# RWKV-7 layer on one core: a reordered recurrence unit, and an output block with two pairs of heads in work

## Chip, cores and metric

One core of a Trainium2 chip runs the whole program. The metric is the device time of one execution in microseconds. TensorE is abbreviated PE in the profile, VectorE DVE, ScalarE ACT, GpSimd POOL, and SyncE, which here issues most DMAs, SP.

## Reference

One layer of a hybrid trunk over 128 context and 512 latent tokens (T = 640 in all), model width 2048: a modulated RMSNorm, one input projection, three token mixers, an output projection, and an expert-choice feed-forward. The change touches the third mixer, RWKV-7 with 16 heads of 64 channels in two directions, and what follows it:

```python
def step(S, xs):                       # per token, per head, per direction
    r_t, w_t, k_t, v_t, a_t, b_t = xs
    sa = jnp.einsum('bhvk,bhk->bhv', S, a_t)
    S = S * w_t[:, :, None, :] + sa[..., None] * b_t[:, :, None, :] + v_t[..., None] * k_t[:, :, None, :]
    return S, jnp.einsum('bhvk,bhk->bhv', S, r_t)
...
o = outs[0] + outs[1]                  # forward + backward
o = ((o - mu) * lax.rsqrt(var + GN_EPS)) * lp['rw_ln_w'] + lp['rw_ln_b']
bonus = jnp.sum(rf * kf * lp['rw_rk'], axis=-1, keepdims=True) * vf
gate = jax.nn.sigmoid(x_g) @ lp['rw_g2']
return ((o + bonus) * gate), finals[0], finals[1]
```

The mean and variance are over the 64 channels of one head. The latent scan starts from a cached state; the context scan's final state is an output.

## The kernel before

The program is a sequence of blocks; a block ends when all engines have done their part. The two that the change touches are `block_rwkv` (the recurrence) and `block_rwkv_output`.

**The recurrence.** Tokens are cut into 10 chunks of 64 (2 context, 8 latent). A unit u is one direction of one pair of heads: 2 x 8 pairs = 16 units. Each engine runs a written-out list, `LINES[u]`, in its own order; semaphores join them. One line holds:

- the front of unit u + 1: jobs `w`, `a` (PE, emptied by ACT with tanh into `sg` and `ar`), then on DVE `scan` (L1593 adds 1 to `sg`, L1595 is a prefix sum over the tokens), then products on POOL (`front`), exponentials on ACT, and the scaled operands `bk` and `aq`;
- the body of unit u: five score jobs `sc` (PE, emptied and masked by DVE L1573 into `sc`), and the inverse of a triangular matrix by doubling, levels 0 to 4, in two halves b: job `x` (needs the transposed tile `tm`, DVE L1565, and `near`, which ACT cuts from `sc` in L1495), job `d`. POOL prepares the tile that is transposed, in three operations (L1312, L1314, L1316, `start`) that wait for the scores of their half. `far` is used at level 4 only;
- 30 slots for the chains of the units u - 2 ("old", chunks 5 to 9) and u - 1 ("new", chunks 0 to 4), alternating. A chunk has three stages: `pw` (PE: five products, four matmul instructions each, of which two need the state `st`; ACT copies `wsb`), `u` (PE, ACT copies `usb`), `z` (PE; then DVE adds the PSUM result to the state into `tmp`, L1631, and scales it by the decay into `st`, L1638; ACT copies the output, L1535). PE starts the next `pw` of that chain only when L1631 has emptied the bank and L1535 has run. When a chain begins, its first `pw` stage has DVE clear `st` (L1626).

The jobs of the body use a ring of four PSUM banks. The order of one line is written in `plan`; its head is: w0 a0 w1 a1, sc0, two slots, sc1, scan, two slots, sc2, two slots, sc3, two slots, sc4, two slots, turn0, x0, slot, bk0, turn1, x1. After the last unit the chains drain: five chunk steps of two chains, then five of one.

**The output block** does the eight pairs one after another. Per pair, 128 partitions x 640 tokens: SP loads `o`, `r`, `k`, `v` (320 KB each) into two buffers; DVE L1797 makes r*rk*k; PE makes the mean; DVE L1799 subtracts it; ACT squares (L1776); PE makes bonus sum, gate and variance; DVE L1801 multiplies bonus by v; ACT takes Ln and Exp (L1779, L1781); DVE L1803 to L1806 finish in four operations; SP stores. PE and DVE begin the next pair when the last one's L1806 is done. Behind pairs 0, 1 and 2, SP also loads three 1 MB slabs of `w_out` each, ahead of the next pair's loads. POOL writes 5 MB of zeros to `ffn` near the start of the block.

Of the kernel before, what the change touches and what calls it, by code (L numbers as in the profile page):

```python
# [15 lines left out]
F32 = mybir.dt.float32  # L16
# [1051 lines left out]
def block_rwkv(nc, z_d, kk_d, par_d, w2, a2, state, ident_d, o_raw_d, state_out):  # L1068
# [17 lines left out]
    def plan(u):  # L1086
# [4 lines left out]
        then = {(0, 1): ["removal"], (2, 0): ["exp_in"], (2, 1): ["exp_inv"], (3, 0): ["exp_ex", "decay", "pad_b"], (3, 1): ["pad_k"], (4, 0): ["pad_a"]}  # L1091
        items = [w0, a0, w1, a1]
        for b in range(NCK // 2):
            items += [("sc", b, u)] + (["scan"] if b == 1 else []) + ["slot", "slot"]
        for lv in range(LAST_LV + 1):
            for k, kind in enumerate(("x", "d")):
                for b in range(2):
                    items += (["turn%d" % b] if (lv, kind) == (0, "x") else []) + [(kind, b, lv, u), "slot"]
                    items += [fill[lv][k]] if lv in fill and b == 0 else []
                items += then.get((lv, k), [])  # L1100
# [35 lines left out]
    with ExitStack() as ctx:  # L1136
# [3 lines left out]
        def sem(name):  # L1140
# [25 lines left out]
        st, tmp, fs, wsb, usb = (sb(n, [P, 2, DH]) for n in ("st", "tmp", "fs", "wsb", "usb"))  # L1166
# [12 lines left out]
        w_done, w_ev, u_done, u_ev, z_done, z_ev, o_ev, s_ready = ([sem(n + str(k)) for k in range(2)] for n in  # L1179
            ("wd", "we", "ud", "ue", "zd", "ze", "oe", "sr"))  # L1180
# [58 lines left out]
        def _(pool):  # L1239
# [33 lines left out]
            for s in (*o_ev, *z_ev, *u_ev, osum_done, o_out, fo_out):  # L1273
                pool.sem_inc(s, 1)

            def front(v):

                pool.wait_ge(cs_done, 3 * v + 2)
# [51 lines left out]
            pool.wait_ge(once_in, 8 * 16)  # L1330
            front(0)
# [3 lines left out]
            for u in range(NU):  # L1335
                for b in range(2):
                    start(u, b)
# [14 lines left out]
        def _(pe):  # L1352
# [64 lines left out]
            def stage(v, i, s):  # L1417
# [7 lines left out]
                if s == "pw":  # L1425
                    if i == 0:
                        emptied([("bk", 2, v), ("vt", 1, v - v % 2), ("sc", NCK // 2 - 1, v)])
                    pe.wait_ge(z_ev[k], q + 1)
                    pe.wait_ge(o_ev[k], q + 1)
                    pe.wait_ge(u_ev[k], q + 1)  # L1430
                    if i == NCP:

                        pe.wait_ge(s_ready[k], q + 1)
                        heads(fv, fs[:, k, :], eye[:], True, True)
                    heads(zv, bktok[:, n, NCK + c, :], vk, True, False, skip_group_check=True)
                    heads(ov, vk, sc[:, n, c, 1, CK:2 * CK], False, False, skip_group_check=True)
# [10 lines left out]
                else:  # L1447
                    pe.wait_ge(u_ev[k], q + 2)
                    heads(zv, bktok[:, n, c, :], usb[:, k, :], False, True, skip_group_check=True)
# [12 lines left out]
        def _(act):  # L1462
# [3 lines left out]
            def empty(key):  # L1466
# [4 lines left out]
                if kind == "w":  # L1471
                    if b == 0:
                        if u:
                            act.wait_ge(pq_done, 3 * u)
                            act.wait_ge(bk_done, 2 * u)
                            act.wait_ge(cs_done, 3 * u)
# [38 lines left out]
            def stage(v, i, s):  # L1515
# [3 lines left out]
                if s == "pw":  # L1519
                    act.wait_ge(w_done[k], q + 1)  # L1520
# [889 lines left out]
```

## Time and profile before

| quantity | value |
|---|---|
| median of 3 runs | 3283.29 us (3275.0 to 3290.36) |
| profiled execution, its own time | 3280.06 us |
| its span | 3278.3 us |
| PE busy in the span | 2821.5 us (86%) |
| DVE busy | 1394.8 us (43%) |
| ACT busy | 533.7 us (16%) |
| POOL busy | 386.7 us (12%) |
| mean granted PE clock | 0.928 of full |
| recurrence block | about 1040 to 1687 us of the span |
| output block | about 1690 to 1820 us |

Busy shares are means over stages with different limits. A group's line names an instruction's line in the kernel; L1366 is the helper that issues nearly all matmuls of the recurrence, so those are told apart by their tiles (`rw_rot` jobs, `rw_wu` and `rw_zo` chain stages).

### The profile page before, as it was taken

Reading aid. Unit: us, or ns where it says so; the run is one execution under the profiler, and the core shown is the slowest. Engines: PE = TensorE matmul, PEld = TensorE weight load, DVE = VectorE, ACT = ScalarE, POOL = GpSimd, SP = SyncE. Lnnn points to the kernel's source line nnn. Section 1 sums busy time; section 2 is a strip of 40 time slices with the busy share of each in tenths; the row PEclk is TensorE's granted clock in tenths of the full one; section 3 lists DMA queues with packets and bytes.
Section 4 is the critical chain, followed back from the end, with each engine's and each line's share of the span. In section 5 each row is a group of like instructions: output and inputs, shape, how many; then the busy total and the mean of one; then the engine's idle time right before and its main releaser. Section 6 shows DMA issues by size and latency. Waiting matters only on the chain. (4 is left out here: it accounts for less than half of the span.)

```text
span 3278.3 us, 66161 instructions
## 1 busy us (share of the span) xinstructions
PE 2821.5 (86%) x28833; PEld 1650.4 (50%) x28833; DVE 1394.8 (43%) x2474; ACT 533.7 (16%) x1318; POOL 386.7 (12%) x499
## 2 busy tenths in 40 slices
PE   5799999999675888888855799959999999999993
PEld 1466676666354788888842345423333233333330
DVE  1676657766343566666623021242223222232223
ACT  2100000000333233333323011110000000000002
POOL 0100000000045334333320000000000000000000
PEclk9899999999777799999977899969999999999996
DMA  9566555553353000011035678859999999999997
GB/s 411 196 201 215 169 204 182 192 204 140 112 136 88 21 23 27 27 34 41 8 150 204 249 268 308 330 196 389 391 411 389 403 394 410 410 411 396 412 419 306
DMA packets 224651, 776.46 MB, mean 237 GB/s; under 512 B 55362, under 2 KB 119577, under 8 KB 155826
## 3 DMA queue, kind: packets, MB, share of 16 engines
q1 hardware_dynamic: 212818, 712.28, 56.3%
q0 software_dynamic: 11248, 60.87, 6.2%
q8 instruction: 175, 2.87, 0.4%
q14 instruction: 42, 0.34, 0.0%
q10 hardware_dynamic: 368, 0.10, 0.0%
HBM read 711.00 MB, written 62.18 MB: 236 GB/s over the span
## 5 line engine op out<-in xcount | busy, mean ns | idle before, releaser
L2144 PE MATMUL ex_ps<-experts_ring,ex_xe 128*32 128x512 f32 (+1 forms) x4608 | 674.9, 600 | 49.5 <-DMA experts_ring<-in_w_up 28.0
L2146 PE MATMUL ex_ps<-experts_ring,ex_xe 128*32 128x512 f32 (+1 forms) x1536 | 674.4, 600 | 0.0
L2144 PEld LDWEIGHTS ex_ps<-experts_ring,ex_xe 128*32 128x32 f32 (+1 forms) x4608 | 214.9, 107 | 494.0 <-issue 476.3
L476 DVE SCALAR_TENSOR_TENSOR pj_macc<-pj_mring,head_cond_t,pj_macc 128x1024 f32<-128x1024 f32 x240 | 296.9, 1278 | 183.1 <-DMA pj_mring<-in_w_ada 183.1
L2159 PE MATMUL ex_ps<-experts_ring,ex_hidt 128*32 128x512 f32 (+1 forms) x2304 | 334.0, 594 | 6.9 <-DVE ex_hidt L2226 6.9
L2161 PE MATMUL ex_ps<-experts_ring,ex_hidt 128*32 128x512 f32 (+1 forms) x768 | 333.5, 594 | 0.0
L549 PE MATMUL pj_ps<-head_hT,head_ring_in 128*128 128x320 f32 x1104 | 312.2, 436 | 6.5 <-DVE head_hT L449 4.2
L1942 PE MATMUL om_ps<-experts_ring,om_ot 128*128 128x512 f32 x640 | 287.7, 611 | 15.1 <-DMA om_ot<-scratch_o 15.1
L2248 DVE SCALAR_TENSOR_TENSOR ex_hid<-ex_hid,ex_gcol,ex_ps 80x512 f32<-80x512 f32 x16 | 11.9, 743 | 592.1 <-ACT ex_hid L2191 592.1
L549 PEld LDWEIGHTS pj_ps<-head_hT,head_ring_in 128*128 128x128 f32 x1104 | 210.8, 191 | 96.6 <-DVE head_hT L449 6.5
L2159 PEld LDWEIGHTS ex_ps<-experts_ring,ex_hidt 128*32 128x32 f32 (+1 forms) x2304 | 107.3, 106 | 224.6 <-issue 216.8
L549 PE MATMUL pj_ps<-pj_t,pj_s 128*128 128x320 f32 x736 | 211.7, 442 | 6.9 <-DVE pj_t L455 6.9
L1942 PEld LDWEIGHTS om_ps<-experts_ring,om_ot 128*128 128x128 f32 x640 | 124.8, 197 | 170.0 <-issue 154.8
L549 PEld LDWEIGHTS pj_ps<-pj_t,pj_s 128*128 128x128 f32 x736 | 141.8, 194 | 73.5 <-issue 11.1
L2146 PEld LDWEIGHTS ex_ps<-experts_ring,ex_xe 128*32 128x32 f32 (+1 forms) x1536 | 162.5, 107 | 0.0
L2226 DVE STREAM_TRANSPOSE ex_xe<-experts_h2t 32x512 f32<-32x512 f32 x192 | 134.7, 702 | 16.9 <-PEq L1819 8.6
L2113 POOL DMA_INDIRECT scratch_ffn<-ex_y,experts_tok x16 | 23.1, 1441 | 992.3 <-ACT ex_y L2202 992.3
L1366 PE MATMUL rw_rot<-rw_tm,rw_near 64*64 64x32 f32 x2560 | 101.2, 222 | 40.4 <-ACT rw_near L1495 38.1
L1366 PE MATMUL rw_rot<-rw_tt,rw_xm 64*64 64x32 f32 x3200 | 126.5, 223 | 2.8 <-DVE rw_xm L1580 2.6
L2191 ACT ACTIVATE ex_hid<-ex_ps 80x512 f32<-80x512 f32 x32 | 17.2, 588 | 674.3 <-PE ex_ps L2146 674.3
L434 ACT COPY pj_stage<-pj_ps 128x320 f32<-128x320 f32 x23 | 9.8, 425 | 684.8 <-PE pj_ps L549 684.8
L1366 PEld LDWEIGHTS rw_rot<-rw_tt,rw_xm 64*64 64x64 f32 x3200 | 116.9, 142 | 4.9 <-DVE rw_xm L1580 4.3
(364 smaller groups left out, 4059.8 us busy)
## 6 DMA issues: line engine op xcount, KB each, us to landing
experts_ring<-in_w_gate SPq DMA_DIRECT2D x128, 1024.0 KB, 20.4
experts_ring<-in_w_up SPq DMA_DIRECT2D x128, 1024.0 KB, 23.4
experts_ring<-in_w_down SPq DMA_DIRECT2D x128, 1024.0 KB, 22.0
experts_ring<-in_w_out SPq DMA_DIRECT2D x68, 1024.0 KB, 7.1
pj_mring<-in_w_ada SPq DMA_DIRECT2D x64, 1024.0 KB, 9.7
head_ring_in<-in_w_in SPq DMA_DIRECT2D x23, 2048.0 KB
ada_ring<-in_w_ada SPq DMA_DIRECT2D x16, 2048.0 KB, 21.4
scratch_z<-pj_stage POOLq DMA_DIRECT2D x19, 640.0 KB, 8.1
```

What stands on the lines that cost most here:

```text
L476: a = nc.vector.scalar_tensor_tensor(acc, w, scalar, acc, ALU.mult, ALU.add)
L549: mm = pe.matmul(bank(name, b)[:, 0:TH], a[:, k, :], h[:, k, :], start=(k == 0), stop=(k == KH - 1))
L1366: mm = pe.matmul(out[rows], lhs[rows], rhs[rows], start=start, stop=stop, **kw)
L1942: mm = pe.matmul(ps[:, banks(t) + h, :], ot[:, t % 2, k, :], w[:, h * 512:(h + 1) * 512], start=(k == 0), stop=(k == KD - 1))
L2113: pool.indirect_dma_start(out=ffn_rows, out_offset=bass.IndirectOffsetOnAxis(ap=tok[:, e:e + 1], axis=0), in_=y[:], in_offset=None, comput ...
L2144: pe.matmul(ps[rows, bank, :], xe[:, k, rows], cols, start=(k == 0), stop=(k == KD - 1))
L2146: mm = pe.matmul(ps[96:96 + rows.stop - rows.start, bank, :], xe[:, k, rows], up[:, g1], start=(k == 0), stop=(k == KD - 1))
L2159: pe.matmul(ps[rows, 3 + c, :], hidt[:, k, rows], w[:, c * 512:(c + 1) * 512], start=(k == 0), stop=(k == 7))
L2161: mm = pe.matmul(ps[96:96 + rows.stop - rows.start, 3 + c, :], hidt[:, k, rows], w[:, 3 * 512:4 * 512], start=(k == 0), stop=(k == 7))
L2191: nc.scalar.activation(hid[0:M, h * 512:(h + 1) * 512], ps[0:M, 2 * h, :], ACT.Silu).then_inc(silu_done, 1)
L2226: tr = nc.vector.transpose(dst[32 * q:32 * q + 32, :, 32 * g:32 * g + 32], src(g, q))
L2248: nc.vector.scalar_tensor_tensor(half, half, gcol[:], up1[:] if h else ps[0:M, 1, :], ALU.mult, ALU.mult).then_inc(hid_done, 1)
```

## The change

In the recurrence: the list of a line is reordered (the first slot stands ahead of sc0, `scan` behind sc0 instead of sc1, the `near` cuts are items of their own and come earlier, the `far` cut moves to level 2). The addition of 1 to `sg` goes from DVE to POOL (`shift`). The state update is one DVE operation instead of two: ACT first makes `ste`, the old state times the decay, in the `pw` stage, and DVE computes z * decay + `ste`. The last chunk of a chain no longer computes z or a new state.

In the output block: three input buffers; the loads of three pairs are issued at once; `w_out` slabs follow behind pairs 2, 3 and 4; pair p's first half is worked together with pair p - 1's second half; r*k goes to POOL without the factor rk, which is folded into the matmul weights (`rk_w`, eight small DVE operations at the start); two pairs of DVE operations are fused, so five remain of seven; each matmul of 640 columns is cut into 320 + 320 instead of 512 + 128; the zeros for `ffn` are written one slab per pair from pair 2 on.

```diff
-        then = {(0, 1): ["removal"], (2, 0): ["exp_in"], (2, 1): ["exp_inv"], (3, 0): ["exp_ex", "decay", "pad_b"], (3, 1): ["pad_k"], (4, 0): ["pad_a"]}
-        items = [w0, a0, w1, a1]
-        for b in range(NCK // 2):
-            items += [("sc", b, u)] + (["scan"] if b == 1 else []) + ["slot", "slot"]
-        for lv in range(LAST_LV + 1):
+        then = {(2, 0): ["exp_in"], (2, 1): ["exp_inv"], (3, 0): ["exp_ex", "decay", "pad_b"], (3, 1): ["pad_k"], (4, 0): ["pad_a"]}
+        items = [w0, a0, w1, a1, "slot", ("sc", 0, u), "scan", "slot"]
+        for b in (1, 2):
+            items += [("sc", b, u), "slot", "slot"]
+        items += [("sc", 3, u), "half0", "slot", "slot", "turn0", ("sc", 4, u), "slot", ("x", 0, 0, u), "slot", "half1", fill[0][0], "slot"]
+        items += ["turn1", ("x", 1, 0, u), "slot", ("d", 0, 0, u), "slot", fill[0][1], ("d", 1, 0, u), "slot", "removal"]
+        for lv in range(1, LAST_LV + 1):
...
+                items += ["far"] if (lv, k) == (2, 0) else []
...
+            def shift(v):
+                pool.wait_ge(act_ev, RANK[G["w", 1, v]])
+                nc.gpsimd.tensor_scalar(sg[:], sg[:], 1.0, None, ALU.add).then_inc(shifted, 1)
...
@@ PE, stage pw
-                    pe.wait_ge(z_ev[k], q + 1)
+                    pe.wait_ge(s_ready[k], q + (i > 0))
@@ ACT, stage pw
+                    if i + 1 < NCK:
+                        e = (ec if i == NCP - 1 else ecp)[:, v % 4, c:c + 1]
+                        act.wait_ge(spread, 3 * v + 1)
+                        act.wait_ge(s_ready[k], q + 1)
+                        nc.scalar.activation(ste[:, k, :], st[:, k, :], ACT.Copy, scale=e)
@@ ACT, stage z
-                    act.wait_ge(z_ev[k], q + 2)
+                    if i + 1 < NCK:
+                        act.wait_ge(s_ready[k], q + 2)
@@ DVE
             def scan(v):
-                dve.wait_ge(act_ev, RANK[G["w", 1, v]])
-                nc.vector.tensor_scalar(sg[:], sg[:], 1.0, None, ALU.add).then_inc(cs_done, 1)
-                dve.wait_ge(cs_done, 3 * v + 1)
+                dve.wait_ge(shifted, v + 1)
                 nc.vector.tensor_tensor_scan(cs[:], reset[:], sg[:], 0.0, ALU.mult, ALU.add).then_inc(cs_done, 1)
...
-                nc.vector.tensor_tensor(tmp[:, k, :], zo[:, k, 0:DH], st[:, k, :], ALU.add).then_inc(z_ev[k], 1)
-                    nc.vector.tensor_tensor(st[:, k, :], tmp[:, k, :], ecp[:, r, c:c + 1].to_broadcast([P, DH]), ALU.mult).then_inc(s_ready[k], 1)
+                    nc.vector.scalar_tensor_tensor(st[:, k, :], z, ecp[:, r, c:c + 1], old, ALU.mult, ALU.add).then_inc(s_ready[k], 1)
@@ output block, SP
+            for p in range(NB):
+                load(p)
             for p in range(NPAIR):
+                if 2 <= p < 2 + RES:
+                    weights(p - 2)
+                sp.wait_ge(done, p + 1)
+                sp.dma_start(o_d[8 + p], o[:, p % NB, :]).then_inc(out, 16)
+                if p + NB < NPAIR:
+                    sp.wait_ge(out, 16 * (p + 1))
+                    load(p + NB)
@@ output block, POOL
+            def bonus_terms(p):
+                pool.wait_ge(loads[p % NB], 64 * (p // NB + 1))
+                if p >= 2:
+                    pool.wait_ge(bonused, p - 1)
+                nc.gpsimd.tensor_tensor(bo[:, p % 2, :], rt[:, p % NB, :], kt[:, p % NB, :], ALU.mult).then_inc(rk_done, 1)
@@ output block, PE, per p of 0..8: mean(p), bonus(p), then var(p-1), gate(p-1)
@@ output block, ACT
+            for p in range(NPAIR + 1):
+                if p < NPAIR:
+                    act.wait_ge(centred, p + 1)
...
+                    nc.scalar.activation(sq[:, p % 2, :], o[:, p % NB, :], ACT.Square).then_inc(squared, 1)
+                if p:
+                    q = p - 1
+                    act.wait_ge(vard, q + 1)
...
+                    nc.scalar.activation(two(rs[:, q % 2, :]), var[:, :, 0:H], ACT.Ln, bias=eps[:]).then_inc(logd, 1)
+                    act.wait_ge(logd, q + 1)
+                    nc.scalar.activation(rs[:, q % 2, :], rs[:, q % 2, :], ACT.Exp, scale=-0.5).then_inc(rsd, 1)
@@ output block, DVE
+            for p in range(NPAIR + 1):
+                if p < NPAIR:
...
+                    nc.vector.tensor_tensor(two(o[:, s, :]), two(o[:, s, :]), mean[:, :, 0:H], ALU.subtract).then_inc(centred, 1)
+                    dve.wait_ge(bonused, p + 1)
+                    nc.vector.tensor_tensor(two(vt[:, s, :]), bonus[:, :, 0:H], two(vt[:, s, :]), ALU.mult).then_inc(weighed, 1)
+                if p:
+                    q, s = p - 1, (p - 1) % NB
+                    dve.wait_ge(rsd, q + 1)
...
+                    ch.link(nc.vector.tensor_tensor(o[:, s, :], o[:, s, :], rs[:, q % 2, :], ALU.mult))
+                    ch.link(nc.vector.scalar_tensor_tensor(o[:, s, :], o[:, s, :], par[:, 24 + q:25 + q], vt[:, s, :], ALU.mult, ALU.add))
+                    dve.wait_ge(gated, q + 1)
+                    nc.vector.scalar_tensor_tensor(two(o[:, s, :]), two(o[:, s, :]), par[:, 32 + q:33 + q], gate[:, :, 0:H], ALU.add, ALU.mult).then_inc(done, 1)
```

## Rows read from the trace of the kernel before

**Rows 1.** Busy us by stage: PE, PEld, DVE, ACT, POOL; granted clock, DMA share, GB/s.

```profile
1057.00:1651.00 594.00, 513.87 (x14284) 486.12 (x14284) 381.73 (x977) 218.50 (x753) 211.22 (x248) 0.94 0.08 25
...
1687.00:1820.00 133.00, 55.83 (x128) 29.17 (x128) 45.37 (x65) 40.67 (x42) 12.94 (x21) 0.71 0.58 219
```

**Rows 2.** Timeline of TensorE: start, length, then idle time before and its releaser.

```profile
1292.04 1.09 PE L1366 MATMUL rw_rot<-rw_aq,rw_bk 64*64 64x128 f32 x16 [0.16 <-ACT rw_sg L1478]
...
1330.58 1.09 PE L1366 MATMUL rw_rot<-rw_aq,rw_bk 64*64 64x128 f32 x16 [0.55 <-ACT rw_sg L1478]
...
1332.54 0.33 PE L1366 MATMUL rw_wu<-rw_st,rw_aq 64*64 64x64 f32 x4
...
1337.71 0.33 PE L1366 MATMUL rw_zo<-rw_vtok,rw_bktok 64*64 64x64 f32 x4 [1.40 <-DVE rw_tmp L1631]
...
1339.32 1.07 PE L1366 MATMUL rw_rot<-rw_aq,rw_bk 64*64 64x128 f32 x16
...
1341.66 0.77 PE L1366 MATMUL rw_rot<-rw_tm,rw_near 64*64 64x32 f32 x20 [1.04 <-ACT rw_near L1495]
...
1345.03 0.77 PE L1366 MATMUL rw_rot<-rw_tm,rw_near 64*64 64x32 f32 x20 [1.41 <-ACT rw_near L1495]
```

**Rows 3.** Timeline of VectorE in the same unit.

```profile
1331.72 0.69 DVE L1573 TENSOR_TENSOR rw_sc<-rw_rot,rw_mask 128x512 f32<-128x512 f32 x1 [1.83 <-PE rw_rot L1366]
...
1332.37 0.11 DVE L1626 MEMSET rw_st<- 128x64 f32 x1
...
1335.10 1.49 DVE L1595 TENSOR_TENSOR_SCAN rw_cs<-rw_reset,rw_sg 128x640 f32<-128x640 f32 x1
...
1337.34 0.85 DVE L1638 TENSOR_TENSOR rw_st<-rw_tmp,rw_ecp 128x64 f32<-128x64 f32 x1
...
1343.29 0.35 DVE L1565 STREAM_TRANSPOSE rw_tm<-rw_tt 128x160 f32<-128x160 f32 x1
```

**Rows 4.** Timeline of ScalarE and GpSimd in the same unit.

```profile
1330.83 0.53 ACT L1478 ACTIVATE rw_sg<-rw_rot,rw_pp 128x320 f32<-128x320 f32 x1
...
1342.74 0.52 POOL L1316 TENSOR_TENSOR rw_tt<-rw_tt,rw_eye 128x160 f32<-128x160 f32 x1
...
1344.84 1.54 POOL L1286 TENSOR_TENSOR rw_qq<-rw_pq,rw_sg 128x640 f32<-128x640 f32 x1
...
1346.38 0.93 POOL L1290 TENSOR_SCALAR rw_kd<-rw_ar,rw_pp 128x640 f32<-128x640 f32 x1
```

**Rows 5.** One operation over the whole trace: count, ns min/median/max, first and last start.

```profile
L1631 DVE TENSOR_TENSOR rw_tmp<-rw_zo,rw_st x160: 184/214/226, 1117.2 to 1684.2; 128x64 f32<-128x64 f32 x160
```

**Rows 6.** Timeline of the output block: VectorE, and the last store.

```profile
1700.39 0.88 DVE L1797 SCALAR_TENSOR_TENSOR ro_bo<-ro_r,ro_par,ro_k 128x640 f32<-128x640 f32 x1 [8.53 <-DMA ro_v<-scratch_z]
...
1724.30 0.89 DVE L1797 SCALAR_TENSOR_TENSOR ro_bo<-ro_r,ro_par,ro_k 128x640 f32<-128x640 f32 x1 [11.12 <-DMA ro_v<-scratch_z]
...
1726.86 0.82 DVE L1799 TENSOR_TENSOR ro_o<-ro_o,ro_mean 128x640 f32<-128x640 f32 x1 [1.67 <-PE ro_mean L1754]
...
1818.25 0.32 SPq L1722 DMA_DIRECT2D scratch_o<-ro_o  x1
```

**Rows 7.** Groups of ScalarE in the output block: count, busy, mean ns, idle before.

```profile
L1779 ACT ACT_TABLE_LOAD x8 | 10.3, 1283 | 0.1
...
L1779 ACT ACTIVATE ro_rs<-ro_var,ro_eps 128x640 f32<-128x640 f32 x8 | 6.3, 793 | 12.8 <-PE ro_var L1754 12.8
...
L1776 ACT ACTIVATE ro_sq<-ro_o 128x640 f32<-128x640 f32 x8 | 5.9, 736 | 66.9 <-DVE ro_o L1799 66.9
...
L1781 ACT ACTIVATE ro_rs<-ro_rs 128x640 f32<-128x640 f32 x8 | 5.9, 736 | 0.1
```

**Rows 8.** DMA issues of the output block: count, KB each, median us to landing.

```profile
scratch_o<-ro_o SPq DMA_DIRECT2D x8, 320.0 KB, 2.2
```

**Rows 9.** Busy time in two stretches, columns as in the first group.

```profile
1710.00:1724.00 14.00, 0.00 (x0) 0.00 (x0) 3.07 (x4) 0.00 (x0) 0.00 (x0) 0.55 1.02 423
...
1308.00:1313.00 5.00, 5.00 (x124) 5.00 (x122) 2.87 (x7) 1.33 (x5) 2.25 (x2) 0.66 0.00 0
```

More of the change, by code:

```diff
@@ L1165, in block_rwkv @@
         s0, fo = sb("s0", [P, 4, DH]), sb("fo", [P, 4, DH])
-        st, tmp, fs, wsb, usb = (sb(n, [P, 2, DH]) for n in ("st", "tmp", "fs", "wsb", "usb"))
+        st, ste, fs, wsb, usb = (sb(n, [P, 2, DH]) for n in ("st", "ste", "fs", "wsb", "usb"))
         of = sb("of", [P, 4, T])
@@ L1696, in block_rwkv_output @@
         zero, zeroed, zero_out = sb("zero", [P, D]), sem("zeroed"), sem("zeroout")
-        once, made, sx_done, ch = sem("once"), sem("made"), sem("sx"), sem("ch")
-        loads = (sem("load0"), sem("load1"))
-        meaned, centred, squared, vard, rsd, rk_done, bonused, done, out = (sem(n) for n in
-            ("meaned", "centred", "squared", "vard", "rsd", "rk", "bonused", "done", "out"))
+        once, made, sx_done, logd = sem("once"), sem("made"), sem("sx"), sem("ch")
+        loads = [sem(f"load{i}") for i in range(NB)]
@@ L1701, in block_rwkv_output, with two, load, weights @@
+        meaned, centred, squared, vard, rsd, rk_done, bonused, weighed, gated, done, out = (sem(n) for n in
+            ("meaned", "centred", "squared", "vard", "rsd", "rk", "bonused", "weighed", "gated", "done", "out"))
+        dch = nc.alloc_semaphore("ro_dch")
         block = ctx.enter_context(nc.Block())
+        def two(t):
+            return t.rearrange("p (h n) -> p h n", n=H)
         @block.sync
         def _(sp):
+            def load(p):
+                for src, dst in ((z_d[ZR + p], rt), (z_d[ZKC + p], kt), (o_raw_d[p], o), (z_d[ZV + p], vt)):
+                    sp.dma_start(dst[:, p % NB, :], src).then_inc(loads[p % NB], 16)
+            def weights(p):
+                sp.dma_start(w_res[:, p, :], w_out[0, p * P:(p + 1) * P, :]).then_inc(res_in, 16)
+                for n in range(2 * p, 2 * p + 2):
+                    load_w_out(sp, w_out, w_ring, ring_in, n, RES)
@@ L1705, in _ @@
             sp.dma_start(par[:], par_d).then_inc(once, 16)
+            sp.dma_start(sx[:], z_d[ZX + 1]).then_inc(once, 16)
             sp.dma_start(g2s[:], g2[0]).then_inc(once, 16)
-            sp.dma_start(sx[:], z_d[ZX + 1]).then_inc(once, 16)
+            for p in range(NB):
+                load(p)
             for p in range(NPAIR):
-                if 1 <= p <= RES:
-                    sp.dma_start(w_res[:, p - 1, :], w_out[0, (p - 1) * P:p * P, :]).then_inc(res_in, 16)
-                    for n in range(2 * (p - 1), 2 * p):
-                        load_w_out(sp, w_out, w_ring, ring_in, n, RES)
-                if p >= 2:
-                    sp.wait_ge(out, 16 * (p - 1))
-                sp.dma_start(o[:, p % 2, :], o_raw_d[p]).then_inc(loads[p % 2], 16)
-                for dst, row in ((rt, ZR), (kt, ZKC), (vt, ZV)):
-                    sp.dma_start(dst[:, p % 2, :], z_d[row + p]).then_inc(loads[p % 2], 16)
-                if p >= 1:
-                    sp.wait_ge(done, p)
-                    sp.dma_start(o_d[8 + p - 1], o[:, (p - 1) % 2, :]).then_inc(out, 16)
@@ L1721, in _ @@
-            sp.wait_ge(done, NPAIR)
-            sp.dma_start(o_d[8 + NPAIR - 1], o[:, (NPAIR - 1) % 2, :]).then_inc(out, 16)
+                if 2 <= p < 2 + RES:
[5 more added lines that the diff above has]
+                    load(p + NB)
             sp.wait_ge(out, 16 * NPAIR)
@@ L1733, in _ @@
                     pool.dma_start(mr[:, cnd, i, :], mod_d[cnd, m * D:(m + 1) * D].rearrange("(k p) -> k p", p=P)).then_inc(crow_in, 16)
-            for t in range(NT):
-                pool.dma_start(ffn_d[t], zero[:]).then_inc(zero_out, 16)
+            nc.gpsimd.memset(zero[:], 0.0).then_inc(zeroed, 1)
+            bonus_terms(0)
+            bonus_terms(1)
             pool.wait_ge(crow_in, 16 * 9)
@@ L1743, in _ @@
                 pool.dma_start(cst_d[cnd].rearrange("i (k p) -> k i p", p=P), mr[:, cnd]).then_inc(crow_out, 16)
+            pool.wait_ge(zeroed, 1)
+            for p in range(2, NPAIR):
+                bonus_terms(p)
+                if p - 2 < NT:
+                    pool.dma_start(ffn_d[p - 2], zero[:]).then_inc(zero_out, 16)
             pool.wait_ge(crow_out, 32)
```

122 lines of the change are left out of this document (63 added, 59 removed).

## Prediction

> **What bounds the kernel now.** I read the busy time by stage first, to see which engine fills each of the two touched blocks. In the recurrence PE works 513.9 of 594 us, the others far less [rows 1]: PE's idle time there, some 80 us, is all that reordering can win. The output block is different: in 133 us no engine reaches half, and DMA moves 219 GB/s on the mean where it moved 423 in a full stretch [rows 1, 9]. That is a chain of waits.
>
> Then the timeline of one recurrence unit. PE has the same holes in every full unit: before sc0, 0.55 (or, in the units of even number, 0.16), waiting for ACT's `sg`; 1.40 before the fourth chunk stage pair, waiting for DVE; 1.04 and 1.41 before x0 and x1, waiting for ACT's `near` cut [rows 2]. I count the 1.40 in all of units 2 to 14 that the view shows. Together 4.0 to 4.4 us of some 36.8 us a unit.
>
> Then the output block. Pair 0's data lands at 1700.39, pair 1's at 1724.30, and the last store is issued at 1818.25 [rows 6]: 94 us for the seven pairs from the second on, 13.4 each.
>
> **Recurrence, unit by unit.** I carry the odd unit through and move only what the new list moves.
>
> 1. The first slot (old chain's `pw`, five groups, about 0.6 us of PE) now stands before sc0, and covers the wait for `sg`. sc0 starts 0.05 later than before, and the hole of 0.55 is PE work now.
> 2. `scan` now sits on DVE between sc0's mask and the second slot, and in the second slot the new chain's first `pw` needs the `st` that DVE clears. Before: mask 1331.72, clear at 1332.37, PE's product with the state at 1332.54 [rows 2, 3]. With the scan between (1.49 long, less the 0.08 by which neighbours on DVE overlap, [rows 3]) the clear comes 1.41 + 0.05 later, and PE stands for as long. The scan itself isn't late: `sg` is complete at 1331.36 and POOL's addition costs 0.93 by the nearest row [rows 4], so 1332.4, when the mask ends as well.
> 3. Behind this the scan is out of the way, so the hole of 1.40 before the second `pw` pair goes: PE would reach it at 1336.3 + 1.46 = 1337.7, where it is today at 1337.71 [rows 2]. A stall is only moved. Value 0 (bounds: -0.5, if POOL is slower than its row, to +1.4, if the clear were not behind the scan).
> 4. That `pw` pair lasts 1337.71 to 1339.32, since the state's second operation runs 0.85 while POOL works [rows 2, 3]. The fused update reads z from PSUM. The nearest row is L1631, also with PSUM: 0.21 in the median and at most 0.23 in 160 runs [rows 5]. I take 0.22, and for the pair its ten groups of four matmuls, 1.17: gain 0.45 (bounds 0 and 0.45).
> 5. x1 waited for `near` to 1345.03, but its transposed tile was ready at 1343.29 + 0.35, so at 1343.70 [rows 2, 3]. The cuts come earlier now; mask of sc4, POOL's three operations (the last ends 1343.26, [rows 4]) and the transpose are the same and come last. Gain 1.33. The hole before x0 isn't a gain of its own: x1 hangs on sc4 by this path alone, and x0 fits into its shadow.
> 6. From x1 on PE's list is as before. ACT has 0.2 more in each of ten stages, under a PE stage of 0.6 (cost 0), and the `far` cut (1.0) ahead of the exponentials in level 2, where `usb` was ready 0.6 to 1.4 before PE took it. Value 0, bound -0.4.
>
> Odd units: 0.45 + 1.33 = 1.78; even ones have 0.39 less of the first hole to fill: 1.39. Six odd and seven even units: 20.4 us. In unit 1 the slots are half as dense and the clear stands in the first slot, ahead of the scan: the hole of 1.75 and the wait for `near` go, about 3.5. Unit 15 has no scan: 1.3. Unit 0: 1.0. The start pays 0.4 (POOL 0.93 for DVE's 0.48 before the first scan).
>
> The drain gains almost nothing. PE resumes a chain after L1631 and the output copy; the update's second operation already lay beside PE's three products that need no state. Last chunk: 0.3.
>
> Sum of the recurrence: 20.4 + 3.5 + 1.3 + 1.0 - 0.4 + 0.3 = 26. Bounds: with -0.9 in each of 13 units 14; with +1.4 there 44.
>
> **Output block.** With two pairs in work the loop is: DVE subtracts (p), ACT squares (p), loads a table, Ln (p-1), loads a table, Exp (p-1), DVE's three last operations (p-1), DVE subtracts (p+1). From rows: 0.82, 0.74, 1.28, 0.79, 1.28, 0.74, then 0.82 and two fused ones at 0.88 [rows 6, 7], 8.2, and 0.4 of handovers: 8.6 a pair instead of 13.4. PE isn't in it: from landed data to the subtraction took 2.56 with the matmuls at the lower clock (1724.30 to 1726.86, [rows 6]), and the variance of p-1 lies beside the square. bonus x v fits into ACT's time.
>
> r*k on POOL costs 1.54 [rows 4] instead of 0.88 on DVE, mostly a pair ahead. But POOL's work can hold DVE's: the state's second operation, two inputs in SBUF, ran 0.85 under it [rows 3], while L1631, one input in PSUM, never grew in 160 [rows 5]. Two of the five DVE operations left have two SBUF inputs. I count two such waits of 1 us on the path, between the 0.6 of [rows 3] and POOL's 1.54. The Trainium skill ("SBUF — State Buffer", section "Who interferes with whom") has it as a rule: a GpSimd operation that reads SBUF and a VectorE one with two SBUF inputs block each other for the whole operation. By that rule, the trace agrees. Were every pair hit at its worst, it would be 8 x 1.54, 12 us instead of 2, which still leaves the block faster.
>
> Times: pair 0 lands at about 1700 as before; pair 1 3.4 us behind, not 24, since no slabs stand before it (1.31 MB a pair at 400 GB/s, a little under the 423 of [rows 9]). Its subtraction is at 1707.2, pair 0 done at 1715.8, then every 8.6: 1724.4, 1733.0, 1742.
>
> From pair 5 on the loads set the pace. SP issues slabs (3.15 MB, 7.5 us at 420 GB/s), waits for the pair, stores it behind the slabs, waits for that store (2.2 landing when nothing is ahead, [rows 8]), then loads. Slabs at 1728.6, store landed 1740 to 1743 (a POOL zero slab, 1.05 MB, 2.5 us, may come between), loads landed 5.3 later. A round is 12.4 to 15 us; pair 7 is the third: landed 1770.5 to 1778. Behind it comes the whole pipe, since ACT squares pair 7 before Ln of pair 6: 2.4 + 5.8 to Exp of 6, 4.1 to Exp of 7, 2.7: 15. Done at 1785.6 to 1793, middle 1789, DVE's hits included. Today 1818.2. Gain 29. Bounds: 40, if the loads keep up (1715.8 + 6 x 8.6 + 4.1 + 3 = 1775 to 1778), and 15, if each round has a whole store and load latency more.
>
> The block after it begins the same way, and the slabs have landed.
>
> **Sum.** 3280.1 (the profiled execution) - 26 - 29 = 3225. The median of the runs is 3.2 above the profiled one: 3227.
>
> **Rivals.**
>
> *The recurrence gets its holes back whole.* If the clear isn't held by the scan, the 1.4 goes too: 13 x 1.4 = 18 more, and the block at its lower bound 11 more: 3198. For it: PE has the idle time [rows 2]. Against: the order on DVE is fixed, and the scan is 1.49 [rows 3]. Chance 0.10.
>
> *The recurrence gains nothing.* The scan's stall, `far` and the added ACT work cost what the cuts give, 26 lost: 3253. For it: the first of these I put at the full size of the hole it replaces. Against: the 1.33 of x1 hangs on nothing that got later. Chance 0.12.
>
> *The output block stays paced by DMA.* SP waits for a landed store behind 3 MB of slabs three times; with 15 us gained instead of 29: 3241. For it: pair 1 today landed 24 us after pair 0 with slabs and zeros ahead [rows 6]. Against: these bytes now move while pairs 2 to 4 compute. Chance 0.15.
>
> *Slower: the stall costs PE its clock.* PE stands about 2 us early in each unit, and could be granted 1.2 GHz behind it. In 1308 to 1313 it had 0.66 of full [rows 9], behind the two holes at x0 and x1, and that unit took 1.5 us longer than its like; the worst, unit 2, 3.6. To eat 55 us it would need 4 us in each of 14 units, more than any unit lost. At 5 us a unit: 3227 + 70 = 3297. Chance 0.03.
>
> **Numbers.** Likeliest, with its own range 3213 to 3241: 0.57; the others as above, 0.03 for what I don't see. The range from the first rival's 3198 to the second's 3253 leaves out the slower case and half of each edge: 3200 to 3254. A measurement here can tell about 0.5%, 16 us, from no change. Faster 0.94, same 0.03, slower 0.03.
>
> **What would show it.** Right: PE's hole before the first state product of a new chain is about 2 us, none of 1.40 before the next pair, and x1 waits for `tm` (L1565), not `near`; L1638's successor never runs 0.8. Pairs 1 to 4 of the output block are done 8.6 apart, with ACT idle only before the square; 5 to 7 wait for loads, 12 to 15 apart; last store near 1763 on the new span (1789 less 26). Wrong: units as long as before, or a clock below 0.9 in them; pairs over 10 us apart with data present; PE waiting for `rk`.

## The result, and the profile after

The changed kernel takes 3256.01 us (median of 7 runs, 3249.61 to 3262.81) where the kernel before takes 3283.32 beside it: ratio 0.9917, 95% interval 0.9893 to 0.9941. That is faster by 27 us. The forecast was 3227, a gain of 56, with a range from 3200; the time lies 2 us above the range. The sign was right, the size half.

The profiled execution took 3255.5 us (span 3253.8, mean granted clock 0.924). To see where the 24.6 us of difference between the two profiled executions lie, I cut the span of every kernel of this study at four events: ScalarE's first write of `sg`; the first VectorE instruction of the output block (the clear of `ro_eps`); the first matmul of the block behind it; the end.

| kernel, profiled execution | recurrence | output block | all behind it | pair 7 done after the output block's start |
|---|---|---|---|---|
| before | 632.8 | 136.6 | 1451.2 | 127.7 |
| changed | 618.6 | 122.9 | 1454.0 | 113.8 |
| forecast for changed | 606.8 | 107.6 | | 98.4 |

Each block gained 14 us, where I had forecast 26 and 29. The stretch behind them is the same code in both, and over all kernels of this study it lay between 1446.9 and 1480.2, by itself more than either gain; nothing here says that the change caused a part of that spread. Below I therefore judge each block by its own length, and the whole by the ratio.

**The recurrence after.** Windows of the changed kernel: busy us of PE, PEld, DVE, ACT, POOL, then granted clock, DMA share, GB/s. The first answers to [rows 1]; the next two are the 3.8 us behind the new stall in two neighbouring units.

```profile
1057.00:1651.00 594.00, 513.45 (x14432) 491.04 (x14432) 366.74 (x827) 250.21 (x917) 242.43 (x265) 0.94 0.08 26
...
1469.50:1473.30 3.80, 3.80 (x48) 3.80 (x50) 0.69 (x1) 0.99 (x4) 0.00 (x0) 0.55 0.17 41
1433.70:1437.50 3.80, 3.80 (x82) 3.60 (x83) 1.77 (x4) 1.23 (x7) 0.55 (x1) 1.00 0.00 0
```

TensorE's timeline in the first of these units (start, length, idle time before and releaser), which answers to [rows 2]:

```profile
1465.18 1.07 PE L1376 MATMUL rw_rot<-rw_aq,rw_bk 64*64 64x128 f32 x16
...
1469.48 0.41 PE L1376 MATMUL rw_wu<-rw_st,rw_aq 64*64 64x64 f32 x4 [2.89 <-DVE rw_st L1641]
...
1469.88 1.93 PE L1376 MATMUL rw_rot<-rw_aq,rw_bk 64*64 64x128 f32 x16
...
1474.88 0.33 PE L1376 MATMUL rw_zo<-rw_vtok,rw_bktok 64*64 64x64 f32 x4
...
1476.07 1.07 PE L1376 MATMUL rw_rot<-rw_aq,rw_bk 64*64 64x128 f32 x16
...
1480.45 0.77 PE L1376 MATMUL rw_rot<-rw_tm,rw_near 64*64 64x32 f32 x20 [1.33 <-DVE rw_tm L1582]
```

VectorE and GpSimd in the same unit, which answer to [rows 3] and [rows 4]:

```profile
1466.29 0.69 DVE L1590 TENSOR_TENSOR rw_sc<-rw_rot,rw_mask 128x512 f32<-128x512 f32 x1 [1.84 <-PE rw_rot L1376]
1467.86 1.49 DVE L1610 TENSOR_TENSOR_SCAN rw_cs<-rw_reset,rw_sg 128x640 f32<-128x640 f32 x1 [0.88 <-POOL rw_sg L1281]
1469.32 0.11 DVE L1641 MEMSET rw_st<- 128x64 f32 x1
...
1479.16 0.28 DVE L1654 SCALAR_TENSOR_TENSOR rw_st<-rw_zo,rw_ecp,rw_ste 128x64 f32<-128x64 f32 x1 [0.82 <-PE rw_zo L1376]
```

```profile
1466.01 1.81 POOL L1281 TENSOR_SCALAR rw_sg<-rw_sg 128x640 f32<-128x640 f32 x1 [3.30 <-ACT rw_sg L1489]
```

The reader should see a chain of three and what follows it. GpSimd's addition takes 1.81 us. VectorE finishes sc0's mask at 1466.98 and stands 0.88 for that addition; then comes the scan, and only then the clear of 0.11 us that TensorE wants. TensorE stands 2.89. Behind it the same 16 matmuls take 1.93 instead of 1.07, at a granted clock of 0.55: mostly the lower of the two levels, 1.2 GHz. In the unit before, a stall of 2.68 left the clock at 1.00.

**The output block after.** VectorE's subtractions of pairs 3 and 5 to 7 and the last operation, which answer to [rows 6]:

```profile
1712.44 0.82 DVE L1851 TENSOR_TENSOR ro_o<-ro_o,ro_mean 128x640 f32<-128x640 f32 x1 [3.13 <-PE ro_mean L1788]
...
1740.32 0.82 DVE L1851 TENSOR_TENSOR ro_o<-ro_o,ro_mean 128x640 f32<-128x640 f32 x1 [8.48 <-PE ro_mean L1788]
...
1759.38 0.82 DVE L1851 TENSOR_TENSOR ro_o<-ro_o,ro_mean 128x640 f32<-128x640 f32 x1 [10.15 <-PE ro_mean L1788]
...
1777.42 0.82 DVE L1851 TENSOR_TENSOR ro_o<-ro_o,ro_mean 128x640 f32<-128x640 f32 x1 [9.60 <-PE ro_mean L1788]
...
1789.82 0.88 DVE L1861 SCALAR_TENSOR_TENSOR ro_o<-ro_o,ro_par,ro_gate 128x640 f32<-128x640 f32 x1
```

SP's queue over one round: the loads of pair 6, slab group 2, the store of pair 4, the loads of pair 7:

```profile
1749.23 0.33 SPq L1728 DMA_DIRECT2D ro_r<-scratch_z  x1
...
1751.03 0.43 SPq L1731 DMA_DIRECT2D experts_ring<-in_w_out  x1
1751.50 0.92 SPq L1689 DMA_DIRECT2D experts_ring<-in_w_out  x2
1752.46 0.55 SPq L1744 DMA_DIRECT2D scratch_o<-ro_o  x1
1767.90 0.33 SPq L1728 DMA_DIRECT2D ro_r<-scratch_z  x1
```

DMA issues of the block (KB each, median us to landing), which answer to [rows 8], and the window over the slow rounds, to [rows 9]:

```profile
experts_ring<-in_w_out SPq DMA_DIRECT2D x9, 1024.0 KB, 9.7
scratch_ffn<-ro_zero POOLq DMA_DIRECT2D x5, 1024.0 KB, 8.5
...
ro_v<-scratch_z SPq DMA_DIRECT2D x8, 320.0 KB, 6.6
```

```profile
1714.00:1768.00 54.00, 22.69 (x57) 13.70 (x56) 16.04 (x19) 18.62 (x20) 6.77 (x6) 0.75 0.89 340
```

Pairs 0 to 3 are done at 24.0, 32.4, 44.7 and 54.9 us after the block's start. Already pair 3 waits for its loads, 3.13 us of idle VectorE. They may go only when pair 0 has left its buffer: from pair 0's last operation its store takes 2.2 to land, the four loads 6.6, and the way to the subtraction 2.7, 11.5 in all, where the computing of a pair takes 8.4. Then pairs 5, 6 and 7 begin 18.8, 19.1 and 18.0 us apart, each behind 8.5 to 10.2 us of idle VectorE, whose matmul waits for data. SP's store of pair 4, 320 KB, is issued at 1752.46 and SP gets past it at 1767.90: 15.4 us.

### The profile page after: what moved, and what is told of

It is laid out like the page before. It is cut to its first block and busy times, and to the rows that moved or that the text cites. A ratio compares the mean times of both kernels' runs of the same rounds, so it can differ in the third digit from the quotient of the medians.

```text
span 3253.8 us, 66031 instructions
## 1 busy us (share of the span) xinstructions
PE 2811.8 (86%) x28705; PEld 1648.3 (51%) x28705; DVE 1365.9 (42%) x2290; ACT 562.0 (17%) x1462; POOL 429.1 (13%) x523
```

## The experiments

Each kernel starts from the changed one; its ratio is to the kernel before, which ran anew beside each group (medians from 3276.26 to 3283.32 us), with the 95% interval. Times of different groups are therefore compared by the ratio.

**The two halves alone.** One kernel takes the changed recurrence with the old output block, the other the reverse.

> The changed recurrence with the old output block. The two profiles put the start of the output block 14 us earlier and its length 13.5 us shorter, so if the halves add up this runs in about 3283 - 14 = 3269 us, 0.9957 of the time before. Rival: the recurrence gives less by itself, and part of the 14 us is a gain in granted clock from elsewhere: 3275 to 3283. The forecast on record (26 us from the recurrence) would want 3257.

> The old recurrence with the changed output block. If the halves add up, 3283 - 13.5 = 3270 us, 0.9959 of before, with the output block 114 us long from its first instruction to the last store's issue. The forecast on record (29 us from the block) would want 3254. If the later blocks pay for the new one (store and slab traffic moved into them), it gives less than 10 us and the time is above 3273.

Measured: changed recurrence alone 3272.67 us, 0.9988 (0.9968 to 1.0008), recurrence 621.7; changed output block alone 3276.76 us, 0.9974 (0.9946 to 1.0001), output block 122.4. By their own lengths both halves are as in the changed kernel (618.6 and 122.9). The whole times say less: the first interval does not hold the 0.9957 that I expected, and both together give 12 us of the 27; where the rest came from, no run shows, and the intervals leave room for most of it. The unchanged recurrence took 642.8 in the second kernel and 632.8 in the profile of before, so 14 us is what one pair of profiles shows, and a gain of 11 to 24 is what these four allow.

**What stands before the clear.** Two edits, one each:

```diff
-        items = [w0, a0, w1, a1, "slot", ("sc", 0, u), "scan", "slot"]
+        items = [w0, a0, w1, a1, "slot", ("sc", 0, u), "slot", "scan"]
```

```diff
-                nc.gpsimd.tensor_scalar(sg[:], sg[:], 1.0, None, ALU.add).then_inc(shifted, 1)
+                nc.gpsimd.tensor_scalar(sg[:], sg[:], 1.0, 1.0, ALU.mult, ALU.add).then_inc(shifted, 1)
```

> The changed kernel with the second slot ahead of scan, so that the clear of the state (0.1 us) stands before the scan (1.5 us) on VectorE. Theory A: TensorE's stall of 2.68 to 2.89 us before the new chain's first state product is the wait for POOL's addition (0.7 to 0.9 us) and the scan (1.5) that stand before the clear. Then this hole goes in all 13 units from 2 to 14. Up to 2.2 us a unit are to be had if nothing else takes its place: 13 x 2.2 = 29, 3256 - 29 = 3227 us. Theory B: the scan, now behind the second slot, delays the next stage's operations instead (front, or the second chain step's update waits for the scan), and the hole comes back at the next pw as the 1.4 us of the kernel before: 13 x 1.2 = 16 us at best, 3240 us. Theory C: TensorE's stall costs nothing because the job list catches up behind it: no change, 3256 us.

> POOL's addition of 1 to sg written with two operations, times 1.0 and plus 1.0, same result. In the traces a POOL tensor_scalar with two operations on 128x640 takes 0.87 to 0.93 us and this one with a single operation 1.81. Theory A: the form sets the price, so it falls to about 0.9, the scan starts with the mask's end, and the stall before the first state product falls from 2.7 to 1.8 to 2.0: 0.8 x 13 = 10 us, about 3246. Theory B: the price comes from what the operation reads or from contention with VectorE, and stays at 1.8: no change, 3256.

Measured: clear ahead of scan 3225.32 us, 0.9835 (0.9802 to 0.9868), recurrence 586.8. Addition with two operations 3244.11 us, 0.9889 (0.9854 to 0.9924), recurrence 610.4. The stall in the two kernels, TensorE's timeline, a fence each:

```profile
1410.18 0.33 PE L1376 MATMUL rw_wu<-rw_st,rw_aq 64*64 64x64 f32 x4 [0.52 <-DVE rw_st L1641]
```

```profile
1432.15 0.33 PE L1376 MATMUL rw_wu<-rw_st,rw_aq 64*64 64x64 f32 x4 [1.92 <-DVE rw_st L1641]
1432.43 1.74 PE L1376 MATMUL rw_rot<-rw_aq,rw_bk 64*64 64x128 f32 x16
```

And the addition over the whole trace (count, ns min/median/max), first in the changed kernel, then with two operations:

```profile
L1281 POOL TENSOR_SCALAR rw_sg<-rw_sg x16: 1812/1814/2373, 1059.5 to 1573.4; 128x640 f32<-128x640 f32 x16
```

```profile
L1281 POOL TENSOR_SCALAR rw_sg<-rw_sg x16: 727/727/1287, 1061.1 to 1567.8; 128x640 f32<-128x640 f32 x16
```

Theory A of both held. The form sets the price, 0.73 against 1.81, and the stall shrinks to 1.92. The addition as such is not to blame: the trace of the kernel before already holds an operation of that size with one arithmetic operation, a multiply in another block, at the same price.

```profile
L863 POOL TENSOR_SCALAR at_qt<-at_qt x4: 1807/1810/1842, 929.4 to 991.0; 128x640 f32<-128x640 f32 x4
```

With the clear ahead the stall is 0.5 in every unit, and the recurrence is 32 us shorter than in the changed kernel, more than the 29 of stall alone. The rest goes with the clock: in the six microseconds behind the stall the granted clock was 1.00 in all 13 units 2 to 14 with the clear ahead. In the changed kernel it was 0.55 to 0.65 (over 3.8 us) in 6 of 13, and with the stall of 1.92 it was 0.71 or 0.72 (over 6 us) in 8 of 13. (With the clear ahead, half speed came at three other places of these units, so not all of the 9 us was won.) So the clock does not simply follow the length of the stall.

**The addition back on VectorE**, in front of the scan there, first with the changed list and then with the clear ahead:

> The changed kernel with the addition of 1 to sg back on VectorE (0.48 us there in the kernel before), directly ahead of the scan; everything else changed. Theory A: the stall before the new chain's first state product is what stands before the clear on VectorE behind sc0's mask: 0.5 + 1.5 us of addition and scan, so 2.3 to 2.5 us in place of 2.7 to 2.9 (1.92 where POOL did it in 0.9). TensorE's half-speed stretch behind every second stall of 2.88 (1.5 us each) should become rarer or stay, by the length of the stall: 3240 to 3256 us. Theory B: the move to POOL is worth something by itself (VectorE's free time): slower than 3256 by 5 us or more.

> The second slot ahead of scan, and the addition of 1 back on VectorE ahead of the scan. Theory A: with the clear out of the way it doesn't matter which engine adds: recurrence of 584 to 587 us as in the two runs with the clear ahead, 3216 to 3225. Theory B: VectorE has no room for the 0.48 us: the next masks and the first update come 0.5 us later in each of 13 units, recurrence of 590 us or more, above 3228.

Measured: 3241.76 us, 0.9894 (0.9854 to 0.9934), stall 2.44, recurrence 607.8; and with the clear ahead 3215.57 us, 0.9787 (0.9754 to 0.9819), recurrence 581.6. The stall behaved by theory A. The lengths say that the move to GpSimd gains nothing and in the form used costs some us; the ratios' intervals overlap, so the whole times can't say it, and 581.6 is even below the 584 to 587 of that theory. With the stall of 2.44, half speed followed in 7 of 13 units. (In the first of these unit 1 was 7 us shorter than in nearly all others, 32.4 us at a mean granted clock of 0.86, where the changed kernel has 39.5 at 0.60; without that it would be some 615, between 610.4 for the stall of 1.92 and 618.6 for that of 2.7 to 2.9.)

> The second slot ahead of scan and POOL's addition with two operations, together. Alone they gave units of 33.0 and 35.2 us (35.8 in the changed kernel). Theory A: with the clear ahead, the addition's price no longer reaches TensorE, so it adds nothing: unit 33.0, time within 5 us of the run with the clear alone, 3225. Theory B: the alternating 1.6 us between units of 32.2 and 33.8 with the clear alone comes from the scan being late for the second chain step; then 0.9 us earlier takes up to 0.8 us off each unit: 32.2, 3215 us.

Measured: clear ahead and two operations together 3215.94 us, 0.9819 (0.9781 to 0.9858), recurrence 583.7. Against 586.8 with the clear alone that is 3 us, within what units differ by clock. The units from 5 on take 33.1 in the mean, and most of them still alternate between 32.0 and 33.4 to 33.7, though the scan starts earlier; that speaks for theory A and against B's reason for the alternation. The median is at B's figure, but a gain of 3 us can't be told from chance here, and its size stays open.

**Filling the stall.** Does idleness bring the low clock, or the place?

```diff
+                    for _ in range(16 if i == 0 and 1 < v < NU - 2 else 0):
+                        heads(uv, sc[:, n, c, 1, 0:CK], vk, True, True)
                     heads(wv, sc[:, n, c, 1, 0:CK], vk, True, False)
```

> The changed kernel with TensorE's stall before the new chain's first state product kept, but filled: in units 3 to 14 it issues 16 groups of four extra matmuls there (about 0.12 us a group, 1.9 us; they write a part of PSUM that is written again before it is read), and the state product still waits for VectorE's clear. Theory A (idle time costs the clock): the granted clock behind the stall stays at 1.00 in all units, the 1.5 us at half speed go from five or six of them, and the recurrence from its first sg to the output block's start is 8 us shorter, 610 in place of 618.6; 3248 us. Theory B (the place or its DMA burst costs the clock, not idleness): alternate units still show 0.55 behind it, 618. Theory C: the extra matmuls only delay: longer than 618.

Measured: 3250.32 us, 0.9887 (0.9851 to 0.9923), recurrence 617.2. Windows of this kernel, columns as above; the first lies behind the filled stall, the second 10 us later, behind TensorE's wait of 1.33 before x1:

```profile
1467.50:1471.30 3.80, 3.80 (x82) 3.61 (x82) 1.77 (x4) 0.85 (x6) 0.51 (x1) 1.00 0.17 40
1478.00:1481.80 3.80, 3.80 (x84) 3.80 (x82) 2.22 (x5) 0.87 (x4) 3.70 (x3) 0.55 0.02 4
```

None of my three theories took this in whole. The extra matmuls did not fill the stall to the end: in most units 0.8 to 1.0 us of it stayed idle. Behind all filled stalls the clock stayed at 1.00, so idleness and not the place brought it down there. But the stretches at half speed were not gone: four came behind the wait before x1 instead, at 1334, 1406, 1478 and 1550, again in every second unit, and the length stayed. Here, filling one hole did not buy the clock back while another was left.

**The rounds of the output block.** Four kernels take one thing each out of what stands in a round.

```diff
# late slabs
-                if 2 <= p < 2 + RES:
-                    weights(p - 2)
+                if NPAIR - RES <= p:
+                    weights(p - NPAIR + RES)
# early slabs
+                if p in (0, 2, 4):
+                    weights(p // 2)
# four buffers, NB = 4; each store signals outs[p % 2]
...
-                if p + NB < NPAIR:
-                    sp.wait_ge(out, 16 * (p + 1))
-                    load(p + NB)
+                if p and p + NB - 1 < NPAIR:
+                    sp.wait_ge(outs[(p - 1) % 2], 16 * ((p - 1) // 2 + 1))
+                    load(p + NB - 1)
# zeros late: all five behind bonus_terms(7)
```

> The changed kernel with the three groups of w_out slabs issued behind pairs 5, 6 and 7 in place of 2, 3 and 4, so that no load of a pair stands behind a slab. Theory A: the rounds of 18.3 to 18.7 us between pairs 4 and 7 are slabs, loads, a store and a zero slab sharing the DMA engines, with SP's wait for that store in between. Then all pairs come 8.4 us apart as pairs 0 to 3 do, the last operation of the block's pair 7 is 114 - 35 = 79 us behind the block's start instead of 114, and what is left of it after the slabs' own landing is a gain of 25 to 30: 3226 to 3231 us. Theory B: the wait is for a store's latency in itself; the rounds stay above 12 us and the gain is below 15. Theory C: the later slabs hold the next block for as long: block shorter, time unchanged.

> The changed kernel with the slabs issued at pairs 0, 2 and 4 in place of 2, 3 and 4. Theory A (bytes in the wrong place): the DMA engines are idle between pair 2's landing (about 1693) and SP's next group (1703 to 1714); moving 3.1 MB there takes one slow round out and puts more room between the other two: pair 7 is done 20 to 30 us earlier, 3226 to 3236 us. Theory B (SP's order): each pair whose store stands behind a slab group still waits 18 us: two such rounds instead of three, 10 us, 3246.

> The changed kernel with four buffers a tensor in place of three; the loads of pair p + 3 are issued behind store p without waiting for it (they wait for store p - 1). Theory A (DMA bytes set the round): slabs 3.15, loads 1.31, store 0.33 and a zero slab 1.05 MB are 5.84 MB a round, 14 us at 420 GB/s, so the rounds fall from 18.5 to about 14: 3 x 4.5 = 13 us, and up to 20 with the head start: 3236 to 3243. Theory B (store latency alone paces SP): the rounds fall to 8.4 and the block shortens by 30 or more: 3226. Theory C: loads are hidden and compute paces: no change.

> The changed kernel with all five zero slabs for ffn issued by GpSimd behind its last product instead of one per pair. Theory A: each round loses its zero slab of 1.05 MB, 2.5 us at 420 GB/s: rounds of 16 in place of 18.5, 7 us less, about 3249; the five slabs then lie beside the 15.9 us between pair 7's landing and the end of the block. Theory B: the rounds are set by latencies, not bytes: no change, 3256, or a few us more where the last store shares with the zeros.

| kernel | us, ratio | pairs 4 to 7 begin apart | pair 7 done | output block |
|---|---|---|---|---|
| changed | 3256.01, 0.9917 | 18.8, 19.1, 18.0 | 113.8 | 122.9 |
| slabs last | 3238.03, 0.9889 (0.9867 to 0.9910) | 11.3, 10.4, 13.0 | 93.2 | 109.6 |
| slabs early | 3251.52, 0.9913 (0.9886 to 0.9940) | 19.0, 8.5, 19.0 | 103.7 | 113.6 |
| four buffers | 3239.06, 0.9898 (0.9866 to 0.9930) | 14.4, 14.1, 13.8 | 98.1 | 108.0 |
| zeros late | 3238.95, 0.9877 (0.9846 to 0.9907) | 13.5, 15.6, 14.0 | 100.9 | 110.2 |

VectorE in the kernel with four buffers:

```profile
1731.99 0.82 DVE L1853 TENSOR_TENSOR ro_o<-ro_o,ro_mean 128x640 f32<-128x640 f32 x1 [5.86 <-PE ro_mean L1790]
...
1746.13 0.82 DVE L1853 TENSOR_TENSOR ro_o<-ro_o,ro_mean 128x640 f32<-128x640 f32 x1 [5.71 <-PE ro_mean L1790]
...
1759.92 0.82 DVE L1853 TENSOR_TENSOR ro_o<-ro_o,ro_mean 128x640 f32<-128x640 f32 x1 [5.35 <-PE ro_mean L1790]
```

With four buffers the round is 14.1, the 5.84 MB that I had counted at 420 GB/s. So I take the changed kernel's round for these bytes and 4 to 5 us of latencies in turn (pair done, store landed, load landed), which three buffers leave uncovered. Zeros late took 4 where I gave it 2.5. Early slabs showed both of its theories: the one round without slabs is 8.5, the two with them stay at 19. Late slabs fell short of the 35 us that I gave them: the pairs come 10.4 to 13.0 apart, not 8.4. With three buffers they could not come 8.4 apart: 11.5 us lie between a pair's end and the subtraction of the pair that takes its buffer, with no slab in the way; so already pairs 2 to 4 were 11.4 and 9.9 apart here. They also give 7 us back: the next block's first matmul comes 16.3 us behind pair 7 and not 9.1. It waits for the load of `om_ot`, which SP issues 9.2 us behind pair 7's end (2.6 in the changed kernel), since the last store now lands behind two groups of slabs. It is the same wait for a small store, moved to the end. As for whole times, none of the four is apart from the changed kernel's ratio by more than the intervals allow; the lengths of the block are.

**Everything spread.** Four buffers, zeros late, and slabs one at a time:

```diff
-                if 2 <= p < 2 + RES:
-                    weights(p - 2)
...
+                for j in {0: (0, 1, 2), 7: ()}.get(p, (p + 2,)):
+                    slab(j)
...
```

> The changed kernel with the changed recurrence and an output block in which the bytes are spread: four buffers, loads that don't wait for the last store, the zero slabs at the end, three w_out slabs behind pair 0 and one behind each of pairs 1 to 6. Theory A: a round then moves 2.7 MB, 6.5 us at 420 GB/s, under the 8.35 us that the chain of ACT and DVE takes for a pair; all pairs come 8.35 apart, pair 7 is done 82 us behind the block's start (113.8 in the changed kernel), the next block starts 91 behind it (122.9): 32 us, 3224. Theory B: a pair can't be paced faster than 10 to 11 us, as in the runs with late slabs or late zeros, because the pieces still collide: block of 93 to 98 us, 3236.

> The spread output block together with the clear ahead of scan and the two-operation addition. Theory A: the two blocks' gains add up: recurrence 32 and output block 32 us less than the changed kernel's 3256: 3192 us, 0.972 of before. Theory B: the rest of the program, bound by TensorE and its granted clock, gives part back: 3200 to 3215.

Measured: 3225.77 us, 0.9836 (0.9803 to 0.9870), pair 7 done at 84.4 (expected 82), output block 99.0 (expected 91; SP gets past the last store 7.0 behind pair 7, with the zeros beside it). The pace fits neither theory: pairs 3 to 7 begin 9.5 to 10.2 apart, not 8.35. Pair 7 is near its time only because the last step, with nothing behind it, takes 4.1. Some of these pairs still wait for their loads: those of pair 4 are issued behind pair 1's last operation and land 7.1 us later, and VectorE stands 1.49. With the clear ahead and the two-operation addition 3198.42 us, 0.9763 (0.9731 to 0.9795): recurrence 584.9, output block 99.0. By the blocks' lengths both gains add up (the whole time, 3198, lies between the 3192 of theory A and the 3200 of B), and this kernel takes 2.4% less than the one before, where the changed one takes 0.8% less.

## Why the prediction was half right

**Recurrence step 1, right.** The first slot covers the wait for `sg`: sc0 has no idle time before it.

**Step 2, the step that failed.** "POOL's addition costs 0.93 by the nearest row [rows 4], so 1332.4, when the mask ends as well" (it adds up to 1332.3), and for steps 2 and 3 together value 0. The nearest row was of the same operation name and shape, but with two arithmetic operations; with one, GpSimd took 1.81. The right row was there to be read, L863 in the kernel before: 1.81. The scan and the clear came 0.7 to 0.9 later than forecast. I had named a bound of -0.5 for this and it was too near. Where the price was as assumed (two operations, 0.73), the stall was 1.92: "about 2 us" was right for that price. Over 13 units the error is 0.8 x 13 = 10 us, and 8.2 is what the two-operation kernel gained in the length of the block.

**The clock, a rival that I gave 0.03 and only as a whole.** In 6 of 13 units TensorE ran the next 3.8 us at about half speed: in the unit at 1469 sc1 to sc3 took 2.14 + 1.83 where the unit before had 1.10 + 1.34, 1.5 us. That is some 9 us in all. The kernel before had such stretches too, two in unit 2, one of them longer, one in unit 3, and two from unit 5 on (at 1308 and 1598). I had priced this mechanism as one that decides the sign or nothing, and it belonged as a term into the sum.

**Steps 3, 4 and 5, right.** There is no 1.40 before the next pair; that pair lasts 1474.88 to 1476.07, 1.19 (forecast 1.17); x1 waits 1.33 for `tm`, not for `near`. The fused update takes 0.28 and not 0.22, inside the same pair. **Step 6, right:** from x1 to the first matmul of the next job `w` are 19.0 us (1480.45 to 1499.45), and 19.05 in the kernel before (1489.55 to 1508.60), so `far` and the added ACT work cost nothing.

Together, in the steady units: 72.0 us for two units before (1442.64 to 1514.64 between two scans), 71.6 after, a gain of 0.4 instead of 3.17. Missing are 1.6 by the longer stalls (2.68 + 2.89 less twice 1.97, which is my 1.46 and the 0.5 that is left with the clear first) and 1.5 by the clock; 0.3 came back elsewhere. Of the 14 that the block gained, 6.1 come from units 2 and 3 (40.6 and 36.6 us before, 36.9 and 34.2 after), where the kernel before had its longest stretches at half speed: a gain that I had not forecast, and that its other profile, with 642.8, shows to vary. That this block still reached my lower bound of 14 is therefore in part luck. Unit 1 gave 1.7 between the scans, not 3.5.

**The start, mis-sized:** 0.4 forecast; the first scan started 1.51 behind `sg` before and 2.96 after, 1.45. With the two-operation addition it was 1.88: 0.4. The same price again.

**Output block, the computing of a pair: right; its pace: only for the first step.** Pair 1 is done 8.4 us behind pair 0 (forecast 8.6), and the tail behind pair 7's landing is 15.9 (forecast 15). But I had "from pair 5 on the loads set the pace"; they did so from pair 3 on, by the 11.5 us above, and pair 3 was done 3.5 us late. The two holds of 1 us by GpSimd did not come in this kernel: VectorE's operations stayed at 0.89 at most. GpSimd's product met one with two SBUF inputs only once, at pair 4, started 0.16 us behind it (1719.98, L1859 at 1719.82), and itself grew, to 2.13 from 1.53. In the kernel with everything spread they came as forecast, twice: L1862 took 1.78 for 0.83 and L1863 2.04 for 0.89. The Trainium skill ("SBUF — State Buffer", section "Who interferes with whom") says that the order of issue decides which of the two engines waits. These traces agree; the one exception is the kernel with the changed output block alone, where VectorE's operation is shown to start 0.03 us first and grew all the same, to 2.24.

**Its round, the second step that failed.** "A round is 12.4 to 15 us; pair 7 is the third: landed 1770.5 to 1778", which is 80 to 87.4 behind the block's start. It landed at 97.9, since the rounds took 18 to 19. I let the slabs run first (7.5), then the store at its unloaded 2.2, then the loads. But slabs, the previous round's loads, the zero slab and the store were in flight together, and the small store landed with the last of them: 15.4 us. The rival "stays paced by DMA" (0.15, a gain of 15) was this case. "These bytes now move while pairs 2 to 4 compute" was true of the bytes and false of the wait: SP's wait for the landed store serialises the next loads behind them.

Both misses were within or beside my bounds for each block (14 and 15), and I took it for unlikely that both would stand at the low end at once. Their causes were separate, and they did. (The forecast's own sum also comes to 3228 and not 3227, which changes nothing.)

## What to carry to other kernels

Before moving a long operation on an engine, list the tiny ones queued behind it: a clear of 0.1 us behind a scan of 1.5 us (and the addition it waits for) cost this kernel's recurrence 32 us, and one swap in a list gave it back. A small transfer that a queue waits for cost here what all bytes in flight beside it cost (15.4 us for one that took 2.2 alone), so price a round by its total bytes plus the latencies in turn, and spread bulk loads so that a round's bytes take less than its computing. When a price is borrowed from another row, the form must match in the number of arithmetic operations too, and a search of the whole trace can find the row that does.

## What the hardware showed that I had not expected

- GpSimd's `tensor_scalar` on 128 x 640 fp32 took 1.81 us with one operation (add) and 0.73 with two (multiply, add), in the median of 16 each.
- Stretches at half speed in every second unit moved to another hole when the first was filled, and nearly kept their number (five behind the stall from unit 5 on, four behind x1's wait). With idle time of 2.0 us a unit (clear ahead) three were left among these units, with 4.1 there were five; the kernel before had 4.4 in smaller pieces, none over 1.41, and two. What decides where they fall stays open.
- The stretch behind the output block, the same code everywhere, took 1446.9 to 1480.2 us in the profiled executions, and 1479.5 and 1480.2 are two of sixteen; each of these was the slowest execution of its kernel's four.
